# Experts' layer: the last token tile by gathered rows, and one-hots by pairs of tokens

## The chip, the cores and the metric

The kernel runs on one NeuronCore of one Trainium2 chip. The metric is the device time of one execution in microseconds. Before the change the median of three runs is 4340.61 us (4338.75 to 4345.99). TensorE (PE) does the matmuls, VectorE (DVE) and ScalarE (ACT) work on tiles, GpSimd (POOL) does small work here, and SyncE (SP) issues the DMAs.

## The reference

512 tokens of width 1024 pass through one hybrid block (windowed attention beside a state space model), a layer of experts, and then two layers of feed-forward, four-way mixer, feed-forward. The change is in the experts' layer. All is fp32. For each token:

```
q = (h @ w_query)                       8 heads x 256
s1, s2 = q halves . keys                128 scores each, by head
v1, i1 = top 16 of s1;  v2, i2 = top 16 of s2
cand = v1 + v2, all 256 pairs;  sc, ci = top 16 of cand
idx = i1[ci / 16] * 128 + i2[ci % 16]   16 experts of 16384 by head
g = softmax(sc)
act = gelu(peer_u[idx] . h) * g         128 picks for each token
out = sum over picks of act * peer_v[idx]
```

## The kernel before

The experts are not gathered. All 16384 are computed for all tokens, in two dense passes, and a matrix of gates (zero where an expert was not picked) is multiplied in between them. Matmul operands are kept as a rounded high part and a low part, and `three` (lines 352 to 356) does three matmuls for each product: high by high, low by high, high by low.

Weights come as items of 512 KB. `load` (L323, on SP) fetches one into one of three raw buffers, `split_ac` (L335, ScalarE) writes the high part, `split_ve` (L345, VectorE) the low part; six pairs of such parts exist, and splitting runs at most four items ahead of TensorE. Engines run their instructions in the order in which they are written, and wait for semaphores in that order.

`Peer` (line 1814) is the layer. `pe_u`, `ac_u`, `ve_u`, `po_u`, `sp_u` write the first pass for each engine, over 144 items: 16 of the query product (`wq`) and 128 of U (128 experts by 1024). For U item j TensorE makes 24 matmuls with the item's part as weights and all 512 tokens as the moving side, ScalarE puts the GELU of the result in a tile (L1957), and SP stores it to `acts` in HBM (L2114). Beside this VectorE picks: `ve_top` (16 best of 128 keys, by head, half and token tile, 64 times), `ve_cand`, `ve_best` (16 best of 256, 32 times; both use `ve_top16`, L1792 to L1796), `ve_places`, `ve_mark` (indices by comparing and summing), the softmax in `ve_soft` and `ve_norm`. Indices and gates are transposed (`turn`, `ve_turned`), and then `ve_gate` builds for eight tokens at a time one-hot rows in fp16: two comparisons (L2081, L2082) and two products (L2085) over 128 x 1024. TensorE multiplies them token by token (`pe_gate`, L1934, two matmuls of 128 columns after each three U matmuls of an item), ScalarE scales the result into a tile (L1982), and SP stores four gates together to `gates` in HBM. There are 64 such gates.

`schedule` decides in which item each of VectorE's units is written: each item brings a budget of time, each kind of unit has a cost, and units are taken in a fixed order until the budget is used. At most one gate is put in an item. The other engines' parts follow from that list.

`pe_v`, `ac_v`, `ve_v`, `sp_v` write the second pass over 128 items of V (128 experts by 1024). `sp_back` fetches an item's activations, `sp_gc` the gates of four items; `ve_prep` multiplies them (L2182), ScalarE rounds the product (`ac_prep`, L2174), `ve_prep` makes the low part (L2184). TensorE uses the activations of each of four token tiles as weights and V as the moving side, two halves of 512 columns, and sums all items in eight PSUM banks. The last four items (`TAIL`) go tile by tile, and before a tile's last item `TileNorm.pe_turn` turns the tile before, for the feed-forward layer's norm. VectorE adds each finished bank to the residual X (L2211) and runs the norm's part of it.

Of the kernel before, what the change touches and what calls it, by code (L numbers as in the profile page):

```python
# [43 lines left out]
def bc(ap, pos, n):  # L44
# [7 lines left out]
SHARED = {"statistics": ("qvar", "kvar", "aovar", "qsd", "ksd", "aosq", "aosd", "gsq", "gsd", "gss", "sqM", "mvar", "msd"),  # L52
          "operands": ("qn", "kn", "kT", "xM", "xTM", "xMT", "xHM", "xLM", "kv0", "SI", "dt", "mag", "gsub", "gexp", "gg")}
# [13 lines left out]
class Dry:  # L67
# [7 lines left out]
    match_replace = affine_select = iota = dma_start = made  # L75
# [461 lines left out]
class TileNorm:  # L537
# [3 lines left out]
    def __init__(self, k, n, gname, XH, XL, mem):  # L541
        self.k, self.n, self.gname, self.XH, self.XL = k, n, gname, XH, XL
        self.D = [mem[:, 128 * i:128 * i + 128] for i in range(4)]

    def pe_turn(self, i):
        k, n, pe, at = self.k, self.n, self.k.pe, self.k.at
        pe.wait_ge(*at("xD", n, i))
        for j in range(8):

            if i == 3 or j % 4 == 0:  # L550
                b = j if i == 3 else 2 * i + j // 4
                o = k.open(b, b + 1, "xT", n, i, j if i == 3 else j // 4)
            c = 0 if i == 3 else 128 * (j % 4)
            pe.e.matmul(o[:, c:c + 128], k.X[:, i, j * 128:(j + 1) * 128], self.D[i], start=True,  # L554
                        stop=True).then_inc(*pe.up("xT", n, i, "column", j))

    def source(self, i, j):
        if i == 3:
            return self.k.got("xT", self.n, i, j)[:, 0:128]
        return self.k.got("xT", self.n, i, j // 4)[:, 128 * (j % 4):128 * (j % 4) + 128]  # L560
# [13 lines left out]
    def ac_upper(self, i, js):  # L574
        k, n, ac, at = self.k, self.n, self.k.ac, self.k.at
        for j in js:
            ac.wait_ge(*at("xT", n, i, "column", j if i == 3 else js[-1]))
# [16 lines left out]
    def ve_lower(self, i, js):  # L594
        k, n, ve, v, at = self.k, self.n, self.k.ve, self.k.ve.e, self.k.at
        for j in js:

            ve.wait_ge(*at("xH", n, i, j if i == 3 else js[-1]))
# [3 lines left out]
            if i == 3:  # L602
                last.then_inc(*ve.free(("xT", n, i, j)))
                ve.note("xL", n, j)
        if i < 3:
            last.then_inc(*ve.free(("xT", n, i, js[0] // 4)))
# [3 lines left out]
    def ac_tile(self, i, done, mem):  # L610
        if i:
            self.ac_upper(i - 1, range(4))
        self.ac_sums(i, done, mem)
        if i:
            self.ac_upper(i - 1, range(4, 8))
        if i == 3:
            self.ac_upper(3, range(8))

    def ve_tile(self, i):
        self.ve_mean(i)  # L620
        if i:
            self.ve_lower(i - 1, range(4))
        self.ve_diag(i)
        if i:
            self.ve_lower(i - 1, range(4, 8))
        if i == 3:
            self.ve_lower(3, range(8))
# [1185 lines left out]

class Peer:
    def __init__(self, k):
# [3 lines left out]
        ar = k.level(3072)  # L1819
        self.TT = [ar(512) for _ in range(3)]  # L1820
        self.I1T, self.I2T = ar(512, dt=HF), ar(512, dt=HF)
        self.GP = ar(2, 512, dt=HF)
        self.IOX = ar(128, dt=HF)
        ar = k.level(20096)
        self.norm, self.next = TileNorm(k, 1, "n2", self.XH, self.XL, self.TT[0]), None
# [3 lines left out]
        ar.at = 1056  # L1829
# [7 lines left out]
        self.S = [ar(4, 128) for _ in range(16)]  # L1837
        self.TMP = ar(256)
        self.MK = ar(8, 16, 16)
        self.CA = self.KT.rearrange("p a b -> p (a b)").rearrange("p (h k) -> p h k", k=256)  # L1840
        k.close()
        self.gd = k.nc.dram_tensor("gates", (16, 128, 128 * 32), F).ap()
        self.ad = k.nc.dram_tensor("acts", (128, 128, 512), F).ap()
        ar = k.level(16384)
        self.GS = [ar(128, 32) for _ in range(2)]
        self.O1 = [ar(8, 128, dt=HF) for _ in range(4)]
        self.O2 = [ar(8, 128, dt=HF) for _ in range(4)]
        self.RH = [ar(2, 8, 128, dt=HF) for _ in range(4)]
        k.close()
        ar = k.level(2 * 2048 + 6 * 512 + 1024)  # L1850
        self.AH, self.AL = k.rounded("AH", 6, 512), k.rounded("AL", 6, 512)
        self.GC = [ar(16, 4, 32) for _ in range(2)]
        self.AI = [ar(512) for _ in range(6)]
        self.mem = ar(1024)
        k.close(3)
        self.schedule()

# [3 lines left out]
    def schedule(self):  # L1861
        units = [("top", c, i) for c in range(16) for i in range(4)]
        for i in range(4):
            units += [("cand", i)] + [("best", i, h) for h in range(8)] + [("places", i)]
            units += [("soft",)] if i == 3 else []
            units += [("mark", i, 0), ("mark", i, 1)]
        units += [("norm",), ("turned",)] + [("gate", n) for n in range(64)]
        cost = {"top": 1.7, "cand": 2.5, "best": 2.4, "places": 2.5, "soft": 0.8, "mark": 7.0, "norm": 1.9,
                "turned": 4.0, "gate": 4.9}
# [3 lines left out]
        time, turn = 0.0, None  # L1873
        for n, (kind, c) in enumerate(self.items):
            time = min(time, 2.0) + (5.0 if kind == "wq" else 4.2)
            while units and time > 0:
                u = units[0]
                if u[0] == "top" and n < u[1] + 2 or u[0] == "turned" and n < turn + 2:
                    break
                if u[0] == "gate" and self.units[n] and self.units[n][-1][0] == "gate":  # L1880
                    break
                time -= cost[u[0]]
                if u[0] == "gate":
                    time += 2.1
# [6 lines left out]
                self.units[n].append(units.pop(0))  # L1891
        assert not units
        self.loads0 = max(n for n, x in enumerate(self.extras) if x) + 4
        assert self.loads0 < len(self.items) - 1, self.loads0

    def pe_u(self):
        k, pe, at = self.k, self.k.pe, self.k.at
        for n, (kind, c) in enumerate(self.items):
# [4 lines left out]
            else:  # L1903
                gates = [x[1] for x in self.extras[n] if x[0] == "gate"]
                pe_proj(k, (kind, c), self.XH, self.XL, 0, 2,
                        between=partial(self.pe_gate, gates[0]) if gates else None)
                if c == 0:
                    self.pe_scores(15)
            for x in self.extras[n]:
                if x[0] == "turn":  # L1910
                    pe.wait_ge(*at("gg"))
                    for m, src in enumerate((self.E1, self.E2, self.GG)):
                        pe_turn(k, [src[:, i, :, :].rearrange("p h k -> p (h k)") for i in range(4)], 128,
                                ("peT", m), 2, 8)

# [10 lines left out]
    def pe_gate(self, n, t):  # L1926
# [6 lines left out]
        for c in range(2):  # L1933
            last = pe.e.matmul(self.gate_bank[:, 128 * (t % 4):128 * (t % 4) + 128], self.O1[n % 4][:, t, :],  # L1934
                               self.RH[n % 4][:, c, t, :], start=c == 0, stop=c == 1)
# [3 lines left out]
    def ac_u(self):  # L1939
        k, ac, at = self.k, self.k.ac, self.k.at  # L1940
        a = ac.e.activation
        for n, (kind, c) in enumerate(self.items):
# [9 lines left out]
            else:  # L1952
# [4 lines left out]
                a(self.TT[c % 3], k.got(("U", c)), ACT.Gelu).then_inc(*ac.free((("U", c),)))  # L1957
                ac.note("pact", c)
            for x in self.extras[n]:
# [4 lines left out]
                if x[0] == "gate":  # L1964
                    self.ac_gate(x[1])

    def ac_scores(self, c):
        k, ac, at = self.k, self.k.ac, self.k.at
        ac.wait_ge(*at("ps", c))
        ac.e.activation(self.S[c].rearrange("p i k -> p (i k)"), k.got("ps", c),  # L1970
# [15 lines left out]

    def po_u(self):
        k, po, at = self.k, self.k.po, self.k.at
        g = po.e
# [3 lines left out]
        po.after().tensor_copy(self.IOX, self.IO)  # L1993
        g.iota(self.IOI, pattern=[[1, 16]], base=0, channel_multiplier=0).then_inc(*po.up())
        po.after().tensor_copy(self.IOF, self.IOI).then_inc(*po.up("iota"))

    def ve_u(self):
# [3 lines left out]
                "gate": self.ve_gate}  # L2001
# [5 lines left out]
    def ve_top(self, c, i):  # L2007
        k, ve, at = self.k, self.k.ve, self.k.at
        ve.wait_ge(*at("psc", c))
        ve_top16(k, self.S[c][:, i, :], self.V12[:, i, c // 2, c % 2, :], self.IXu[:, i, c // 2, c % 2, :],  # L2010
                 self.TMP[:, 0:128]).then_inc(*ve.up())
# [31 lines left out]

    def ve_soft(self):
# [6 lines left out]
    def ve_norm(self):  # L2051
# [6 lines left out]
        ve.after().tensor_tensor(gg3, gg3, bc(sm, 2, 16), ALU.mult).then_inc(*ve.up("gg"))  # L2058

    def ve_turned(self):  # L2060
        k, ve, v, at = self.k, self.k.ve, self.k.ve.e, self.k.at
        GT, GR = self.QT
        for n, dst in enumerate((self.I1T, self.I2T)):
            ve.wait_ge(*at("peT", n))
            v.tensor_copy(dst, k.got("peT", n)).then_inc(*ve.free(("peT", n)))
        ve.wait_ge(*at("peT", 2))
        v.tensor_scalar(GT, k.got("peT", 2), GSCALE, None, ALU.mult).then_inc(*ve.free(("peT", 2)))
# [5 lines left out]
    def ve_gate(self, n):  # L2073
        k, ve, v, at = self.k, self.k.ve, self.k.ve.e, self.k.at
        o1, o2, rh = self.O1[n % 4], self.O2[n % 4], self.RH[n % 4]
        s = slice(8 * n, 8 * n + 8)
# [1728 lines left out]
```

## Time and profile before

| what | value |
|---|---|
| runs, median of 3 | 4340.61 us |
| profiled execution | span 4340.4 us; the page gives no other time for it |
| granted TensorE clock, mean of the records | 0.960 |
| TensorE busy | 4130.1 us, 95% |
| VectorE busy | 2287.0 us, 53% |
| ScalarE busy | 1404.0 us, 32% |
| GpSimd busy | 189.6 us, 4% |
| DMA | 473.59 MB, mean 109 GB/s |

Busy times of engines overlap. Times are microseconds from the first instruction unless marked ns. A matmul's duration is its passage through the array, and successive ones overlap, so the distance of two starts, not the duration, says what one costs. Instructions are named by the line of the kernel that wrote them, and a helper's line stands for all who call it.

### The profile page before, as it was taken

How to read it: one execution, taken by the hardware profiler on the slowest of the kernel's cores; microseconds unless marked ns; L12 is line 12 of the kernel's file. 1: busy time of each engine (PE TensorE's matmuls, PEld its weight loads, DVE VectorE, ACT ScalarE, POOL GpSimd, SP SyncE). 2: the span in 40 equal slices, each digit the busy share in tenths (PEclk: the TensorE clock that was granted, in tenths of full speed). 3: DMA queues.
4: the chain of work that ended last, by engine and by line, in shares of the span. 5: the costliest groups of instructions: out<-in, count | busy, mean ns of one | idle time of the engine just before them, and what ended most of it. 6: DMA issues, size and time to landing. Idle time of an engine off the chain costs nothing. (4 is left out here: it accounts for less than half of the span.)

```text
span 4340.4 us, 47785 instructions
## 1 busy us (share of the span) xinstructions
PE 4130.1 (95%) x19325; PEld 3249.6 (75%) x19325; DVE 2287.0 (53%) x3707; ACT 1404.0 (32%) x2380; POOL 189.6 (4%) x356
## 2 busy tenths in 40 slices
PE   9789999999999999999999988899999999789999
PEld 7767887666678888888878765788778787657877
DVE  5748888777724444444332776433243338754332
ACT  3444223333333333333222433422232233333221
POOL 8500000000000000000000000000000000000000
PEclk9779999999999999999999987999999999889999
DMA  3012444555566666662332210233323322102332
GB/s 124 1 39 88 127 138 132 178 185 176 177 193 201 189 187 188 190 194 83 94 96 77 78 51 1 73 96 94 97 78 93 97 78 73 36 1 93 97 97 73
DMA packets 253388, 473.59 MB, mean 109 GB/s; under 512 B 15904, under 2 KB 138944, under 8 KB 250992
## 3 DMA queue, kind: packets, MB, share of 16 engines
q1 hardware_dynamic: 253072, 470.45, 35.5%
q8 instruction: 153, 2.51, 0.2%
q14 instruction: 67, 0.55, 0.0%
q10 hardware_dynamic: 96, 0.08, 0.0%
HBM read 399.96 MB, written 70.52 MB: 108 GB/s over the span
## 5 line engine op out<-in xcount | busy, mean ns | idle before, releaser
L345 DVE TENSOR_TENSOR wlast<-wraw,wlast 128x1024 fp32r<-128x1024 f32 x406 | 496.2, 1226 | 762.7 <-ACT wlast L335 762.2
L354 PE MATMUL ps<-XH,wlast 128*128 128x512 f32 (+1 forms) x1888 | 779.5, 413 | 0.0
L356 PE MATMUL ps<-XH,wlast 128*128 128x512 f32 (+1 forms) x1888 | 747.2, 396 | 0.0
L355 PE MATMUL ps<-XL,wlast 128*128 128x512 f32 (+1 forms) x1888 | 746.5, 395 | 0.0
L335 ACT ACTIVATE wlast<-wraw 128x1024 fp32r<-128x1024 f32 x406 | 426.6, 1055 | 403.5 <-PE ps L356 389.2
L345 DVE TENSOR_TENSOR wtwo<-wraw,wtwo 128x1024 fp32r<-128x1024 f32 x212 | 260.1, 1228 | 438.4 <-ACT wtwo L335 437.9
L356 PEld LDWEIGHTS ps<-XH,wlast 128*128 128x128 f32 x1888 | 357.4, 189 | 86.8
L354 PEld LDWEIGHTS ps<-XH,wlast 128*128 128x128 f32 x1888 | 358.1, 190 | 75.4 <-issue 5.2
L355 PEld LDWEIGHTS ps<-XL,wlast 128*128 128x128 f32 x1888 | 358.8, 190 | 70.6
L354 PE MATMUL ps<-XH,wtwo 128*128 128x512 f32 x960 | 397.5, 414 | 0.0
L356 PE MATMUL ps<-XH,wtwo 128*128 128x512 f32 x960 | 381.8, 398 | 0.0
L355 PE MATMUL ps<-XL,wtwo 128*128 128x512 f32 x960 | 381.7, 398 | 0.0
L335 ACT ACTIVATE wtwo<-wraw 128x1024 fp32r<-128x1024 f32 x212 | 223.7, 1056 | 245.4 <-PE ps L356 239.4
L356 PE MATMUL ps<-wlast,AL 128*128 128x512 f32 x672 | 264.7, 394 | 0.0
L355 PE MATMUL ps<-wlast,AH 128*128 128x512 f32 x672 | 263.4, 392 | 0.0
L354 PE MATMUL ps<-wlast,AH 128*128 128x512 f32 x672 | 260.8, 388 | 0.0
L1957 ACT ACTIVATE arena<-ps 128x512 f32<-128x512 f32 x128 | 76.5, 598 | 566.6 <-PE ps L356 566.6
L356 PEld LDWEIGHTS ps<-XH,wtwo 128*128 128x128 f32 x960 | 183.0, 191 | 43.9
L355 PEld LDWEIGHTS ps<-XL,wtwo 128*128 128x128 f32 x960 | 183.9, 192 | 35.7
L354 PEld LDWEIGHTS ps<-XH,wtwo 128*128 128x128 f32 x960 | 183.5, 191 | 35.8
L2336 ACT ACTIVATE HH<-arena 128x512 fp32r<-128x512 f32 x88 | 55.6, 632 | 419.3 <-DVE arena L2354 419.3
L2354 DVE TENSOR_TENSOR arena<-arena,ps 128x512 f32<-128x512 f32 x88 | 60.4, 687 | 245.1 <-PE ps L356 245.1
(476 smaller groups left out, 6801.0 us busy)
## 6 DMA issues: line engine op xcount, KB each, us to landing
wraw<-in_ut SPq DMA_DIRECT2D x128, 512.0 KB, 4.2
wraw<-in_v SPq DMA_DIRECT2D x128, 512.0 KB, 3.9
wraw<-in_ffn_gate SPq DMA_DIRECT2D x88, 512.0 KB, 3.5
wraw<-in_ffn_up SPq DMA_DIRECT2D x88, 512.0 KB, 3.5
wraw<-in_ffn_down SPq DMA_DIRECT2D x88, 512.0 KB, 3.5
acts<-arena SPq DMA_DIRECT2D x128, 256.0 KB, 4.5
gates<-arena SPq DMA_DIRECT2D x16, 2048.0 KB, 9.0
arena<-gates SPq DMA_DIRECT2D x32, 1024.0 KB, 7.9
```

Of the source, the lines that this page charges most:

```text
L335: ac.e.activation(W.items[n][7], W.rawof(n), ACT.Copy).then_inc(*ac.up("whi", n))
L345: ve.e.tensor_tensor(W.items[n][8], W.rawof(n), W.items[n][7], ALU.subtract).then_inc(*ve.up("wlo", n))
L354: mm(out, lh, rh, start=start, stop=False)
L355: mm(out, lh, rl, start=False, stop=False)
L356: return mm(out, ll, rh, start=False, stop=stop)
L1957: a(self.TT[c % 3], k.got(("U", c)), ACT.Gelu).then_inc(*ac.free((("U", c),)))
L2336: a(self.HH[:, f, :], s, ACT.Copy).then_inc(*ac.up("hh", *id, f))
L2354: v.tensor_tensor(s, s, k.got((*id, "up", f)), ALU.mult).then_inc(*ve.free(((*id, "up", f),)))
```

## The change

Three of the four token tiles (384 tokens) stay in the dense passes. The U matmuls go over 384 columns, V uses three tiles of activations, the GELUs, stores and fetches shrink to 384 tokens, and there are 48 gates for 64. The last tile (tokens 384 to 511) is done by its picks: its indices are computed first; GpSimd issues 128 indirect DMAs that fetch for each of the 128 tokens the row of U of its x-th pick (128 rows of 4 KB, 512 KB), and 128 more that fetch the rows of V, into five buffers in turn. VectorE multiplies each row by the token's normalised activations and sums (a "dot", 128 of them); ScalarE takes the GELU in four chunks of 32; VectorE multiplies by the gates and adds each V row, scaled, to one of two accumulators, X itself and `XN` (a "row", 128 of them). One of those 128 only scales its row.

The scores' buffers shrink from 16 to 8. The one-hot rows are laid out by pairs of tokens, [4 pairs, 128, 2], and `O2` is a single buffer. `schedule` has new costs and budgets, puts dots between gates and after them, and a second list (`later`) puts what remains of dots and the rows into the items of the V pass; what is left at the end is written after its last item. In the feed-forward's norm the gathered tile is turned first, before the last item of the first dense tile. Semaphores of some more events are shared by name.

```diff
+DENSE, GATHERED, PICKS = 3, 3, 128
+TOKENS = 128 * DENSE
...
+    ROWS, SCORES, CHUNK = 5, 8, 32
+    GATES = TOKENS // 8
...
+        units = [("top", c, i) for c in range(16) for i in range(4)] + [("rows",)]
+        for i in (GATHERED, 0, 1, 2):
...
+            units += [("index",)] if i == GATHERED else []
+        units += [("norm",), ("turned",)] + [("gate", n) for n in range(self.GATES)]
+        cost = {"top": 1.7, "rows": 1.3, "cand": 2.5, "best": 2.4, "places": 2.5, "soft": 0.8, "mark": 7.0,
+                "index": 0.3, "norm": 2.1, "turned": 3.5, "gate": 2.9, "dot": 1.3}
...
-            time = min(time, 2.0) + (5.0 if kind == "wq" else 4.2)
+            time = min(time, 2.0) + (4.4 if kind == "wq" else 3.0)
...
+                wait = u[0] == "top" and n < u[1] + 2 or u[0] == "turned" and n < turn + 2
+                if wait or u[0] == "gate" and self.units[n] and ("gate", u[1] - 1) in self.units[n]:
+                    u = ("dot", dots)
+                if u[0] == "dot" and (known is None or n < known + 4 or dots == PICKS):
                     break
...
+        later = [("dot", x) for x in range(dots, PICKS)] + [("act", c) for c in range(PICKS // self.CHUNK)]
+        later += [("row", x) for x in range(PICKS)]
...
+            time = min(time, 1.0) + 1.78
...
+                time -= 0.4 if u[0] == "act" else 1.28
...
+        self.later[127] += later
...
+    def pe_expert(self, c, gate):
...
+            last = three(k, o, wh[:, j, :], wl[:, j, :], self.XH[:, j, 0:TOKENS], self.XL[:, j, 0:TOKENS], j == 0,
+                         j == 7)
...
+        for n in range(2 * PICKS):
+            if n >= self.ROWS:
+                m = n - self.ROWS
+                po.wait_ge(*(at("dot", m) if m < PICKS else at("row", m - PICKS)))
+            x = n % PICKS
+            g.indirect_dma_start(out=self.RB[n % self.ROWS], out_offset=None, in_=tables[n // PICKS],
+                                 in_offset=bass.IndirectOffsetOnAxis(ap=self.PLACE[:, x:x + 1], axis=0)).then_inc(
...
+    def ve_dot(self, x):
...
+        ve.wait_ge(*at("gathered", x))
+        ve.wait_ge(*at("xn"))
+        v.tensor_tensor_reduce(out=rows, in0=rows, in1=self.XN, scale=1.0, scalar=0.0, op0=ALU.mult, op1=ALU.add,
+                               accum_out=self.DOT[:, x:x + 1]).then_inc(*ve.up("dot", x))
...
+    def ve_row(self, x):
...
+            acc = self.XN if x % 2 else k.X[:, GATHERED, :]
+            v.scalar_tensor_tensor(acc, rows, w, acc, ALU.mult, ALU.add).then_inc(*ve.up("row", x))
...
+        def pairs(x):
+            return bc(x[:, s].rearrange("p (t u) -> p t u", u=2), 2, 128)
...
+        v.tensor_tensor(o2, io, pairs(self.I2T), ALU.is_equal).then_inc(*ve.up("o2", n))
...
-                if j == 127 and i:
-                    self.next.pe_turn(i - 1)
+                if j == 127:
+                    self.next.pe_turn(self.next.order[i])
...
+            for u in self.later[j]:
+                does[u[0]](*u[1:])
+        x = k.X[:, GATHERED, :]
+        ve.wait_ge(*at("row", PICKS - 1))
```

## Rows read from the trace of the kernel before

**Rows 1.** The page, its busy times and one line of 40 slices in tenths.

```profile
PE 4130.1 (95%) x19325; PEld 3249.6 (75%) x19325; DVE 2287.0 (53%) x3707; ACT 1404.0 (32%) x2380; POOL 189.6 (4%) x356
...
DVE  5748888777724444444332776433243338754332
```

**Rows 2.** Windows: length, busy of each engine (instructions), granted clock, DMA share, GB/s.

```profile
447.00:730.00 283.00, 279.60 (x1214) 222.93 (x1213) 245.15 (x543) 80.87 (x104) 0.00 (x0) 0.99 0.48 136
730.00:1203.00 473.00, 459.62 (x2560) 291.27 (x2560) 361.28 (x313) 161.93 (x257) 0.00 (x0) 1.00 0.55 176
...
1287.00:1990.00 703.00, 703.00 (x3054) 573.25 (x3053) 323.18 (x394) 219.23 (x271) 0.00 (x0) 1.00 0.61 185
```

**Rows 3.** The line of the U pass's GELUs: durations, first and last start.

```profile
L1957 ACT ACTIVATE arena<-ps x128: 597/598/602, 454.8 to 1283.1; 128x512 f32<-128x512 f32 x128
```

**Rows 4.** Order of time in a U item: start, length, instruction.

```profile
560.21 0.40 PE L356 MATMUL ps<-XH,wtwo 128*128 128x512 f32 x1
560.44 0.39 PE L354 MATMUL ps<-XH,wtwo 128*128 128x512 f32 x1
```

**Rows 5.** Order of time in an item with a gate.

```profile
902.44 0.29 PE L1934 MATMUL ps<-arena 128*128 128x128 f16 x2
...
903.33 0.28 PE L1934 MATMUL ps<-arena 128*128 128x128 f16 x2
```

**Rows 6.** Order of time where matmuls are narrower, of 16 and of 256 columns.

```profile
69.94 0.26 PE L354 MATMUL ps<-XH,wtwo 128*128 128x16 f32 x1
...
70.06 0.26 PE L355 MATMUL ps<-XL,wtwo 128*128 128x16 f32 x1
...
2527.91 0.28 PE L354 MATMUL ps<-wlast,XH 128*128 128x256 f32 x1
...
2529.08 0.28 PE L355 MATMUL ps<-wlast,XH 128*128 128x256 f32 x1
```

**Rows 7.** Order of time in the V pass.

```profile
1499.63 0.39 PE L356 MATMUL ps<-wlast,AL 128*128 128x512 f32 x1
1499.86 0.39 PE L354 MATMUL ps<-wlast,AH 128*128 128x512 f32 x1
```

**Rows 8.** VectorE's groups by form: busy, mean ns, idle before; gates, then V pass.

```profile
L2085 DVE TENSOR_TENSOR arena<-arena 128x1024 f16<-128x1024 f16 x106 | 124.8, 1219 | 0.0
...
L345 DVE TENSOR_TENSOR wlast<-wraw,wlast 128x1024 fp32r<-128x1024 f32 x71 | 87.0, 1225 | 161.8 <-ACT wlast L335 161.8
...
L2184 DVE TENSOR_TENSOR AL<-arena,AH 128x512 fp32r<-128x512 f32 x106 | 73.4, 692 | 74.1 <-ACT AH L2174 74.1
```

**Rows 9.** Order of time on VectorE: starts of two successive bests, two successive tops.

```profile
501.75 0.43 DVE L1792 MAX8 arena<-arena 128x8 f32<-128x256 f32 x1
...
504.12 0.43 DVE L1792 MAX8 arena<-arena 128x8 f32<-128x256 f32 x1
...
457.65 0.29 DVE L1792 MAX8 arena<-arena 128x8 f32<-128x128 f32 x1
...
459.35 0.29 DVE L1792 MAX8 arena<-arena 128x8 f32<-128x128 f32 x1
```

**Rows 10.** Waits in the V pass: total us, times, longest.

```profile
DVE AL L2184 <- ACT AH L2174: 74.1, 106, 0.7
```

**Rows 11.** DMA: V pass, 10 us slices of U's gates, 5 us of U, landing, issue.

```profile
q1 hardware_dynamic: 86458, 112.13, 63.1%
...
DMA packets 86486, 112.52 MB, mean 191 GB/s; under 512 B 3855, under 2 KB 59151, under 8 KB 86458
...
GB/s 126 207 202 136 212 184 144 224 168 136 247 159 120 272 154 102 286 154 87 293 154 79 301 146 80 303 143 80 318 129 86 322 118 94 339 94 103 336 88 110
...
817.00:822.00 5.00, 5.00 (x28) 3.06 (x27) 3.13 (x4) 2.52 (x4) 0.00 (x0) 1.00 1.08 455
...
wraw<-in_v SPq DMA_DIRECT2D x107, 512.0 KB, 3.9
...
1501.09 0.33 SPq L323 DMA_DIRECT2D wraw<-in_v  x1
```

More of the change, by code:

```diff
@@ L1836, in __init__ @@
         self.QT = [ar(512) for _ in range(2)]
-        self.S = [ar(4, 128) for _ in range(16)]
+        at_s = ar.at
+        self.S = [ar(4, 128) for _ in range(self.SCORES)]
         self.TMP = ar(256)
+        ar.at = at_s
         self.MK = ar(8, 16, 16)
@@ L1890, in schedule @@
                     self.extras[n].append(u)
-                self.units[n].append(units.pop(0))
+                if u[0] == "index":
+                    known = n
+                if u[0] == "dot":
+                    dots += 1
+                    if dots % self.CHUNK == 0:
+                        self.extras[n + 1].append(("gelu", dots // self.CHUNK - 1))
+                    self.units[n].append(u)
+                else:
+                    self.units[n].append(units.pop(0))
         assert not units
-        self.loads0 = max(n for n, x in enumerate(self.extras) if x) + 4
+        gates = [n for n, x in enumerate(self.extras) if any(u[0] in ("turn", "gate") for u in x)]
+        self.loads0 = max(gates) + 4
         assert self.loads0 < len(self.items) - 1, self.loads0
+        later = [("dot", x) for x in range(dots, PICKS)] + [("act", c) for c in range(PICKS // self.CHUNK)]
+        later += [("row", x) for x in range(PICKS)]
+        self.later, self.gelus, time, gelu = [[] for _ in range(128)], [[] for _ in range(128)], 0.0, 0
+        for j in range(128):
+            time = min(time, 1.0) + 1.78
+            while later and time > 0:
+                u = later[0]
+                if u[0] == "act" and u[1] == PICKS // self.CHUNK - 1 and j < gelu + 2:
+                    break
+                time -= 0.4 if u[0] == "act" else 1.28
+                if u[0] == "dot" and u[1] % self.CHUNK == self.CHUNK - 1:
+                    self.gelus[j].append(u[1] // self.CHUNK)
+                    gelu = j
+                self.later[j].append(later.pop(0))
+        self.later[127] += later
     def pe_u(self):
@@ L2000, in ve_u @@
                 "soft": self.ve_soft, "mark": self.ve_mark, "norm": self.ve_norm, "turned": self.ve_turned,
-                "gate": self.ve_gate}
+                "gate": self.ve_gate, "rows": self.ve_rows, "index": self.ve_index, "dot": self.ve_dot}
         for n, item in enumerate(self.items):
@@ L2147, in pe_v @@
             pe.wait_ge(*at("al", j))
-            for i in range(4):
+            for i in range(DENSE):
                 for n in range(2):
@@ L2153, in pe_v @@
         ws = {j: k.W.pair(("V", j)) for j in range(TAIL, 128)}
-        for i in range(4):
+        for i in range(DENSE):
             for j, w in ws.items():
@@ L2200, in ve_v @@
         k, ve, v, at = self.k, self.k.ve, self.k.ve.e, self.k.at
+        does = {"dot": self.ve_dot, "act": self.ve_act, "row": self.ve_row}
         for j in range(self.LEAD):
@@ L2206, in ve_v @@
                 self.ve_prep(j + self.LEAD)
-        for i in range(4):
+            for u in self.later[j]:
+                does[u[0]](*u[1:])
+        x = k.X[:, GATHERED, :]
+        ve.wait_ge(*at("row", PICKS - 1))
+        for n in range(2):
+            s = slice(512 * n, 512 * n + 512)
+            v.tensor_tensor(x[:, s], x[:, s], self.XN[:, s], ALU.add).then_inc(*ve.up("x+", "peer", GATHERED, n))
+        self.next.ve_tile(0)
+        for i in range(DENSE):
             for n in range(2):
@@ L2266, with __init__ @@
     TAIL = 18
-    def __init__(self, k, name, l, gname, norm, before):
+    def __init__(self, k, name, l, gname, norm, before, order=(0, 1, 2, 3)):
         self.k, self.id, self.norm_n, self.before = k, (name, l), norm, before
@@ L3676, in build @@
         plan_ffn(k, "ffn1", l)
-        stages.append(Ffn(k, "ffn1", l, f"f1{l}", norm, before))
+        stages.append(Ffn(k, "ffn1", l, f"f1{l}", norm, before, (0, 1, 2, 3) if l else (GATHERED, 0, 1, 2)))
         plan_mixer(k, l)
```

232 lines of the change are left out of this document (146 added, 86 removed).

## The prediction

> **What bounds the kernel now.** I read the page's first two parts, then the windows cut at the stages of the experts' layer, then TensorE's order of time inside each stage, and last VectorE's groups, waits and the DMA view of the same stretches. The page gives TensorE 95% and VectorE 53% of the span [rows 1]. By windows, the layer's first expert pass (product with U) is PE-busy at 97 to 99% and the second pass (V, 1287 to 1990 us) at 100%; VectorE has 87% in the picking stretch, 76% in the gates' and 46% in the V pass [rows 2]. So TensorE's stream sets the time everywhere here, with VectorE close behind in the picking stretch. The 128 U items run from the GELU at 454.8 to that at 1283.1: 828.3/127 = 6.52 us each, 835 us in all [rows 3]. A U matmul of 512 columns starts 0.23 us after the one before, 24 x 0.2333 = 5.6 us an item [rows 4]; the 64 items with a gate then take (835 - 64 x 5.6)/64 = 7.45 us, and the order of time shows a step of 0.88 us for three U matmuls and two gate matmuls [rows 5]. V steps at 0.229 us, 5.5 us an item, 704 us for 128 [rows 7].
>
> **TensorE's part.** U keeps 24 matmuls an item, but each goes over 384 columns for 512. No such row exists. Matmuls of 256 columns step at 0.117 us (the two rows are ten starts apart, 1.17 us), and those of 16 columns at 0.112: that is the floor of the weight load [rows 6]. 384 lies above the floor, so I interpolate between 0.117 and 0.2333: 0.175 us, 4.2 us an item (bounds 0.16 and 0.19). V keeps 512 columns and drops a quarter of its matmuls: 18 x 0.229 = 4.13 us an item. 16 gates of 64 go. By TensorE alone: U 80 x 4.2 + 48 x (4.2 + 1.85) = 628 us for 835 (-207); V 529 for 704 (-175). The page "TensorE: Matmul & The Clock Gate" (LDWEIGHTS) of the Trainium skill gives columns/1.2 ns for a weight load, 107 ns here; rows [rows 6] have 112 ns, and by either the load hides under 384 columns.
>
> **VectorE's part, U.** Splitting an item is 1.23 us. The planner's new costs, added up: 64 tops of 1.7 and four times (2.5 + 8 x 2.4 + 2.5 + 2 x 7.0) are 262 us, with the small units 267; 14 query items take 4.4 each, the rest (205) fills U items at 3.0, so picking ends at U 68 and gates 0 to 47 stand at U 69 to U 116, one each. Dots of 1.3: 2 before them, (3.0 + 0.8 - 2.9)/1.3 = 0.7 an item among them, 32 in whole units, and 26 in the last 11 items; 60 in all, and 68 remain for the V pass. Before the gates, its budget of 3.0 plus the split gives 4.23 us an item, as much as TensorE's 4.2. The plan's costs fit what rows show: a top of 128 takes 1.70 us, a best of 256 2.37 [rows 9]. A balance with no slack, and lumps of 7 us (the mark), will leave TensorE waiting now and then; I take 4.4 us for these 69 items: 304 us (bounds 4.2 and 4.7). Gate items: four one-hot operations took 1.22 us each over 1024 fp16 elements [rows 8]; the innermost step of zero becomes a run of two. If that makes VectorE take two elements a step, each costs what 512 elements cost, 0.69 us [rows 8], a gate 2.8 us; with the split and 0.67 dots, 4.8 us, under TensorE's 6.05. If it does not, 1.23 + 4.9 + 0.8 = 6.9 us and 48 x 0.85 = +41 us. I take the fast form. The Trainium skill, "Vector Engine (DVE) Microarchitecture Reference" (Performance modes — why throughput varies by op and dtype), says the pairing mode wants 2-byte operands with step one innermost, and that a single element read again runs at one a cycle: the 1.22 us rows agree with the second half. The gates' operands now lie two elements apart for TensorE; as a full-floor load of 0.112 us each [rows 6], 0.22 a pair where the step now leaves 0.88 - 0.70 = 0.18, they would cost 384 x 0.05 = 19 us, and nothing if the distance does not count; I take 0. The last 11 U items want 2.4 dots each: 56 us with some waiting. U comes to 304 + 291 + 56 = 651, **-184 us**.
>
> **VectorE's part, V.** Per item: the split 1.14 (start to start), multiply and subtract over 384 columns 0.55 each for 0.69 [rows 8], the wait for ScalarE's rounding between them, 74.1/106 = 0.7 now [rows 10], 0.6 then. The plan's 1.78 us an item at 1.28 a unit put 177 units into the 128 items (68 dots, 109 row sums), 1.38 an item. A dot or row sum over 1024 fp32 from two SBUF tiles is like the split, 1.15 to 1.25 us: 1.66. Sum 4.5 us: more than TensorE's 4.13, so VectorE becomes the bound. In its queue the split, multiply and subtract stand behind each gather's wait, and ScalarE's split and TensorE behind those.
>
> **The DMA.** Each gather moves 128 rows of 4 KB, 0.52 MB. A V item carries V 0.52, activations 0.20, gates 0.20 and 1.38 gathers 0.72: 1.64 MB. Now the stage runs 191 GB/s at 63% busy, 302 GB/s if full: 5.4 us. The U pass shows 10 us slices of 339 GB/s (4.8 us) and 5 us at 455 (3.6 us) [rows 11]. The nearest row for 4 KB rows is the slice of 339. With 4.5 by VectorE and 4.8 by DMA I take 4.75 us: 608 us (bounds 4.13 and 5.7).
>
> **The tail.** 19 row sums are left after the last item, and the gathered tile is now the first that TensorE turns: it waits in front of the last item's matmuls for 19 sums x 1.15, two additions and the norm's chain of some 4 us. Nothing covers that, as TensorE is not ahead: **+25 us** (bounds 10 and 60, the latter if gathers pace the sums). V: 608 + 25 for 704, **-71 us**.
>
> **What a gather costs to issue** no row shows. SP issues a transfer in 0.33 us, and one of 512 KB lands 3.9 us after issue [rows 11]. So 0.4 us if descriptors are cheap, 3.9 if gathers do not overlap at all (five buffers say they should), more than that if GpSimd needs long for the 128 places. The plan leaves 608/177 = 3.4 us. I take under 3.1, hidden. The Trainium skill, "SBUF — State Buffer" (Who interferes with whom), speaks against the change: descriptors of a DMA from GpSimd are written by its cores, which share ports with VectorE; it gives 0.62 us alone and 3.1 us beside a VectorE copy. An estimate by that figure: 196 x 3.1 = 608 us for V, the same as mine, and 25 us more in U's last items. No run here shows it yet.
>
> **Sum.** 4340.4 - 184 - 71 = 4085, and about 3 for the index, the normalised row tile (1.2 like a split) and the copy of the gates, which stand in the full picking stretch: **4088 us**. The span of the profiled execution, 4340.4, is the only time the page gives for it; the median run is 4340.61, so I add nothing.
>
> **Rivals.**
> (a) Gathers pace both passes: with g us each, in order on one engine, U's last items take 26g and V 196g in all (19 of them in the tail). The change is 835 - 595 - 26g + 704 - 196g = 944 - 222g us: nothing at 4.25 us, and slower beyond. For it: one issue has 128 places to look up, where SP's 0.33 us deals with one regular block; and each must follow the dot or row five before it. Against: five buffers in flight, and 4.25 us is more than the 3.9 from issue to landing of a transfer of that size. At g = 4.8, 4340 + 122 = 4462. At 3.9 us (serial transfers) 4262.
> (b) The 16 DMA engines become the bound at the stage's present 302 GB/s: V 128 x 5.44 = 696, + 25, so -184 + 17 + 3: 4176. For it: the share of 63% already; against: the 455 GB/s.
> (c) Nothing but TensorE binds: 4340 - 207 - 175 + 25 = 3984. For it: present waits are nearly all other engines' waits for TensorE. Against: the 4.5 us above.
> (d) The pairs do nothing for VectorE: +41, 4129; inside the main range.
>
> **Chances.** Forecast with (d), 4040 to 4140: 0.46. (b) and near it, 4140 to 4220: 0.21. (c), 3960 to 4040: 0.10. Serial gathers, 4220 to 4300: 0.08. (a) slower: 0.13; level: 0.02. This kernel's measurement tells 0.2%, 9 us, from nothing. Faster 0.85, same 0.02, slower 0.13. Range 3990 to 4290: it leaves out (a) and the best of (c).
>
> **What would show it.** After the change: U matmul starts 0.175 us apart; gate operations near 0.69 us; no VectorE wait for gathers in U before its last 11 items; V items of 4.75 us with PE near 87% and VectorE over 90%; a stall of TensorE of some 25 us before the last item, ended by the norm's diagonal; 256 gathers at under 3.1 us. The prediction is wrong if VectorE's top wait in V is a DMA with its steps over 3.4 us, or if U items before the gates exceed 4.7 us.

## The result and the profile after

The changed kernel takes 4078.94 us (median of 4 runs, 4076.54 to 4082.92) against 4339.68 us for the one before (4333.4 to 4345.99): a ratio of 0.9393, 95% interval 0.9377 to 0.9410. The profiled span is 4075.3 us for 4340.4.

First the page after, busy times, VectorE's slices and the DMA's rate; answers to [rows 1].

```profile
PE 3770.3 (93%) x18298; PEld 3085.7 (76%) x18298; DVE 2367.9 (58%) x4034; ACT 1348.4 (33%) x2352; POOL 552.5 (14%) x612
...
DVE  5746898877677888743337764332333266933332
...
GB/s 125 9 26 94 128 190 178 231 285 285 346 354 344 346 353 343 270 88 93 98 78 74 48 1 73 93 93 98 78 94 96 95 75 55 18 37 83 93 99 73
```

The windows after, columns as in [rows 2]: picking, gates, the last U items, V items, the layer's tail.

```profile
447.00:732.00 285.00, 285.00 (x1618) 285.00 (x1617) 259.54 (x586) 101.69 (x140) 6.30 (x5) 1.00 0.57 174
732.00:1030.00 298.00, 297.19 (x2064) 236.64 (x2063) 234.40 (x341) 123.71 (x204) 41.53 (x41) 1.00 0.82 280
1030.00:1085.00 55.00, 33.81 (x175) 32.85 (x173) 30.87 (x47) 11.07 (x16) 26.19 (x20) 0.81 0.97 354
1085.00:1640.00 555.00, 511.66 (x2144) 402.85 (x2145) 447.94 (x590) 175.12 (x240) 250.29 (x162) 0.99 0.97 348
1640.00:1700.00 60.00, 26.00 (x108) 19.47 (x106) 49.71 (x51) 13.26 (x18) 33.96 (x25) 0.80 0.92 330
```

TensorE is still full in the U pass up to 1030 us. In the V pass it has 92%, VectorE 81%, and the DMA engines 97% at 348 GB/s, where the pass before ran at 185 [rows 2]. In the tail TensorE has 43%, and its granted clock is 0.80 on the mean: it fell from 2.4 to 1.2 GHz while TensorE stood (0.51 in 1676 to 1715 us, and still 0.50 in the first matmuls after it, 1718 to 1724).

The lines that bound the passes after: U's GELUs (answers to [rows 3]) and the roundings of V's activations; each with durations, first and last start.

```profile
L2020 ACT ACTIVATE arena<-ps x128: 490/492/495, 453.3 to 1081.3; 128x384 f32<-128x384 f32 x128
...
L2315 ACT ACTIVATE AH<-arena x128: 522/525/527, 1084.3 to 1675.2; 128x384 fp32r<-128x384 f32 x128
```

U items take 628.0/127 = 4.94 us for 6.52, so the pass loses 202 us. V items take 590.9/127 = 4.65 us. From the last GELU to the last addition to X, V pass and tail together, it was 1283.1 to 2001.7 us before and is 1081.3 to 1739.2 after: 61 us less. The two make 263 of the 265 us between the spans.

Matmuls in order of time after, two of U, two of gates; answers to [rows 4, 5].

```profile
600.10 0.34 PE L357 MATMUL ps<-XH,wlast 128*128 128x384 f32 x1
600.28 0.34 PE L358 MATMUL ps<-XL,wlast 128*128 128x384 f32 x1
...
900.19 0.29 PE L1996 MATMUL ps<-arena 128*128 128x128 f16 x2
...
900.90 0.29 PE L1996 MATMUL ps<-arena 128*128 128x128 f16 x2
```

A 384-column matmul starts 0.176 us after the last (ten rows of the same stretch, 600.10 to 601.87). The step with two gate matmuls is 0.71 us, of which the pair takes 0.18, as it did before (0.88 - 0.70).

VectorE's groups from 300 to 1750 us: split, dot, row sum, one-hot, low part (answers to [rows 8]).

```profile
L348 DVE TENSOR_TENSOR wlast<-wraw,wlast 128x1024 fp32r<-128x1024 f32 x185 | 225.2, 1220 | 63.2 <-ACT wlast L338 62.8
L2151 DVE CUSTOM_DVE_ANT_0 arena<-arena 128x1024 f32<-128x1024 f32 x128 | 154.3, 1221 | 8.3 <-DMA arena<-in_u,arena 8.2
...
L2174 DVE SCALAR_TENSOR_TENSOR X<-arena,X 128x1024 f32<-128x1024 f32 x64 | 82.0, 1281 | 2.5 <-DMA arena<-in_v,arena 2.4
...
L2325 DVE TENSOR_TENSOR AL<-arena,AH 128x384 fp32r<-128x384 f32 x128 | 71.5, 559 | 75.6 <-ACT AH L2315 75.6
...
L2225 DVE TENSOR_TENSOR arena<-arena 128x1024 f16<-128x1024 f16 x96 | 61.8, 686 | 0.0
```

The one-hot operation fell from 1219 to 686 ns. VectorE waited for gathered rows 8.2 us in all dots and 7.0 in all row sums: they come in time.

TensorE's waits from 1000 to 1740 us: what waited, for whom, us in total, times, longest.

```profile
PE ps L357 <- DVE AL L2325: 53.9, 52, 4.4
PE ps L558 <- DVE arena L590: 45.3, 1, 45.3
PE ps L357 <- ACT arena L2020: 17.4, 2, 16.8
```

Three costs are new: V items held by VectorE's low parts, the norm's first turn (L558) behind the row sums, and one stop near the end of the U pass.

That V queue in order of time, an item with one row sum and an item with two:

```profile
1640.58 1.22 DVE L348 TENSOR_TENSOR wtwo<-wraw,wtwo 128x1024 fp32r<-128x1024 f32 x1
...
1641.71 0.55 DVE L2323 TENSOR_TENSOR arena<-arena 128x384 f32<-128x384 f32 x1
...
1642.85 0.56 DVE L2325 TENSOR_TENSOR AL<-arena,AH 128x384 fp32r<-128x384 f32 x1 [0.59 <-ACT AH L2315]
1643.33 1.28 DVE L2174 SCALAR_TENSOR_TENSOR X<-arena,X 128x1024 f32<-128x1024 f32 x1
1644.53 1.22 DVE L348 TENSOR_TENSOR wlast<-wraw,wlast 128x1024 fp32r<-128x1024 f32 x1
...
1647.28 1.28 DVE L2174 SCALAR_TENSOR_TENSOR arena<-arena 128x1024 f32<-128x1024 f32 x1
1648.47 1.28 DVE L2174 SCALAR_TENSOR_TENSOR X<-arena,X 128x1024 f32<-128x1024 f32 x1
1649.67 1.22 DVE L348 TENSOR_TENSOR wlast<-wraw,wlast 128x1024 fp32r<-128x1024 f32 x1
```

From split to split: 3.95 us with one sum, 5.14 with two, so at 1.38 an item 3.95 + 0.38 x 1.19 = 4.40 us without any wait for a DMA. The items take 4.65. The rest is a wait for a DMA, and not one for gathered rows. VectorE's longest waits from 1000 to 1740 us:

```profile
DVE AL L2325 <- ACT AH L2315: 75.6, 128, 0.6
DVE arena L2323 <- DMA arena<-acts: 36.4, 25, 3.4
```

The first is in the 4.40 already. The second, for the activations that SP fetches, is 36.4/128 = 0.28 us an item, and 4.40 + 0.28 = 4.68: full DMA engines reach TensorE through VectorE's queue.

The DMA view from 1150 to 1700 us (queues with packets, MB, share of 16 engines; landings), answers to [rows 11]:

```profile
q1 hardware_dynamic: 74126, 102.29, 53.7%
q0 software_dynamic: 23986, 87.33, 42.8%
...
wraw<-in_v SPq DMA_DIRECT2D x108, 512.0 KB, 7.1
...
arena<-in_v,arena POOLq DMA_INDIRECT x123, 7.6
```

### The profile page after: what moved, and what is told of

Read it like the earlier page. It is cut to its first block and busy times, and to the rows that moved or that the text cites. A ratio compares the mean times of both kernels' runs of the same rounds, so it can differ in the third digit from the quotient of the medians.

```text
span 4075.3 us, 46458 instructions
## 1 busy us (share of the span) xinstructions
PE 3770.3 (93%) x18298; PEld 3085.7 (76%) x18298; DVE 2367.9 (58%) x4034; ACT 1348.4 (33%) x2352; POOL 552.5 (14%) x612
## 5 line engine op out<-in xcount | busy, mean ns | idle before, releaser
L357 PE MATMUL ps<-XH,wlast 128*128 128x512 f32 (+2 forms) x1888 | 734.0, 389 | 17.4 <-ACT arena L2020 17.4
L359 PE MATMUL ps<-XH,wlast 128*128 128x512 f32 (+2 forms) x1888 | 708.4, 375 | 0.0
L358 PE MATMUL ps<-XL,wlast 128*128 128x512 f32 (+2 forms) x1888 | 707.8, 375 | 0.0
L357 PE MATMUL ps<-XH,wtwo 128*128 128x512 f32 (+1 forms) x960 | 374.5, 390 | 0.0
L358 PE MATMUL ps<-XL,wtwo 128*128 128x512 f32 (+1 forms) x960 | 362.5, 378 | 0.0
L359 PE MATMUL ps<-XH,wtwo 128*128 128x512 f32 (+1 forms) x960 | 362.2, 377 | 0.0
L2080 POOL DMA_INDIRECT arena<-in_u,arena x128 | 172.0, 1344 | 783.7 <-DVE arena L2151 547.1
L357 PE MATMUL ps<-wlast,AH 128*128 128x512 f32 x504 | 202.2, 401 | 33.2 <-DVE AL L2325 33.1
L2080 POOL DMA_INDIRECT arena<-in_v,arena x128 | 193.8, 1514 | 212.2 <-DVE X L2174 99.3
L2315 ACT ACTIVATE AH<-arena 128x384 fp32r<-128x384 f32 x128 | 67.2, 525 | 402.2 <-DVE arena L2323 402.2
```

The source lines that it names most:

```text
L357: mm(out, lh, rh, start=start, stop=False)
L358: mm(out, lh, rl, start=False, stop=False)
L359: return mm(out, ll, rh, start=False, stop=stop)
L2080: g.indirect_dma_start(out=self.RB[n % self.ROWS], out_offset=None, in_=tables[n // PICKS], in_offset=bass.IndirectOffsetOnAxis(ap=self.PL ...
L2315: ac.e.activation(self.AH[:, j % 6, :], self.AI[j % 6], ACT.Copy).then_inc(*ac.up("ah", j))
```

## The experiments

Three theories stood for V items of 4.65 us: VectorE's queue, the DMA engines, or GpSimd's gathers. Each edit is against the changed kernel unless it says otherwise.

**Without the gathered tile's work.** No gathers; the dots and row sums are left out, and one memset clears the dots' results.

```diff
-        for n in range(2 * PICKS):
+        for n in range(0):
...
-        v.tensor_tensor_reduce(out=rows, in0=rows, in1=self.XN, ...)
-            v.scalar_tensor_tensor(acc, rows, w, acc, ...)
+        ve.note("row", x)
```

> The changed kernel without its gathers, dots and row sums: the last token tile gets nothing from its experts. This is TensorE's own gain. If only TensorE binds where nothing else does, the V items fall from 4.65 us (first to last rounding of the activations, 1084.3 to 1675.2 us) to 18 x 0.229 = 4.13, 66 us less; the 45 us stall before the norm's first turn goes to under 5; the 17 us stall at the end of the U pass, where SP sends eight fetches in a row, shrinks to under 8 if the gathers' bytes cause it and stays at 17 if the fetches alone do. Sum: 4079 - 66 - 42 - 10 = about 3960 us. Rival: V items stay over 4.4 us because of SP's own transfers or VectorE's multiply and subtract; then about 3990.

Measured: 3947.4 us, ratio to before 0.9100 (0.9074 to 0.9126). The first to the last rounding in V is 1064.2 to 1579.2, 4.06 us an item, and 4.15 between items 16 and 112: TensorE's pace. The stop of 16.8 us is gone, and the norm's waits are 4.2 us. So a quarter off the dense passes is worth 392 us, and the picks' own work gives 132 us back.

**Narrow V rows.** The same number of gathers, a quarter of the bytes.

```diff
-        tables = (k.d["u"], k.d["v"].rearrange("a b d -> (a b) d"))
+        tables = (k.d["u"], k.d["v"].rearrange("a b (q d) -> (a b q) d", q=4))
...
-            g.indirect_dma_start(out=self.RB[n % self.ROWS], ...
+            cut = 1024 if n < PICKS else 256
+            g.indirect_dma_start(out=self.RB[n % self.ROWS][:, 0:cut], ...
```

> The V rows are gathered 256 columns wide instead of 1024 (from a view of V in which the same indices fall on other quarter rows); as many gathers of 128 rows, as many row sums over 1024 columns, the gathered tile's sums are of stale data. The DMA engines carry 1.09 gathers' worth of bytes less an item once rows begin. Theory DMA (16 DMA engines bound the V items, 1.64 MB at 353 GB/s = 4.65 us): V items with rows fall to TensorE's 4.13 or VectorE's 4.4; the second half of the V pass gains 0.3 to 0.5 us an item, 80 items: 25 to 40 us, and the tail's stall 5 to 15 us: 4025 to 4050. Theory VectorE (split, multiply, wait for ScalarE, subtract, 1.38 dots or rows in one queue = 4.4 us, and only 0.26 of 4.65 is waiting for DMA): gains at most 0.26 x 80 = 21 us and nothing in the tail, whose 24 sums are VectorE's own: 4058 to 4070. Theory GpSimd (each gather 1.5 us of descriptor work paces): no change, 4079.

**Narrow row sums.** Full gathers, sums over 256 columns.

```diff
+        rows = rows[:, 0:256]
...
-            acc = self.XN if x % 2 else k.X[:, GATHERED, :]
+            acc = (self.XN if x % 2 else k.X[:, GATHERED, :])[:, 0:256]
```

> Row sums over 256 columns for 1024, gathers unchanged: the gathered tile's result lacks the rest. A row sum falls from 1.28 to about 0.45 us. Theory VectorE: its queue falls from 4.4 to 3.3 us in items with rows, so TensorE's 4.13 or the DMA takes over; 80 items gain 0.3 to 0.5 us, 25 to 40 us, and the tail of 24 sums loses 15 to 20 us: 4020 to 4040. Theory DMA: the V items stay at 4.65 us and the tail, paced by gathers of 0.52 MB, gains under 8: 4070 to 4079. Theory GpSimd: no change.

**Both.**

> The two edits narrow_rows and narrow_sums together: V rows gathered 256 wide, sums over 256 columns. Each alone took V items in the half with row sums from 4.75 to 4.4 and 4.5 to 4.7 us. Theory two bounds side by side (VectorE's queue 4.4, the DMA engines about 4.6): with both gone the items with row sums fall to TensorE's 4.15, as without gathers, 75 items x 0.27 below narrow_rows, and the norm's stall of 36 us to 15: 4050 - 20 - 20 = 4010. Rival: GpSimd's 128 indices a gather (1.5 us each) or latency paces the rest; then items stay at 4.4 and the total at 4035 to 4045.

Windows in the half of the V pass with row sums (from 1340 us), one line from each kernel: as changed, narrow rows, narrow sums, both. Where VectorE waits there for the activations' fetch, that row stands below; with narrow rows it has none, and with both it has waited 3.1 us in all.

```profile
1340.00:1640.00 300.00, 273.12 (x1145) 213.71 (x1144) 244.10 (x280) 94.29 (x128) 138.27 (x89) 0.99 0.98 350
...
DVE arena L2323 <- DMA arena<-acts: 18.0, 14, 3.4
```

```profile
1340.00:1640.00 300.00, 289.22 (x1227) 228.16 (x1226) 259.81 (x299) 100.23 (x136) 149.88 (x95) 1.00 0.81 250
```

```profile
1340.00:1640.00 300.00, 281.25 (x1174) 223.57 (x1174) 183.59 (x288) 96.66 (x132) 122.21 (x92) 0.98 1.00 360
...
DVE arena L2324 <- DMA arena<-acts: 77.2, 28, 7.2
```

```profile
1340.00:1600.00 260.00, 260.00 (x1131) 211.97 (x1130) 181.49 (x286) 100.60 (x129) 104.45 (x91) 1.00 0.88 277
```

Measured: narrow rows 4049.4 us (0.9334, 0.9312 to 0.9356), narrow sums 4050.5 (0.9338, 0.9313 to 0.9364), both 4014.2 (0.9241, 0.9225 to 0.9256). Narrow rows came out at the edge of the DMA theory's forecast, and narrow sums between the forecasts of the two theories, so neither holds alone. Over sixteen items at a time, from the starts of the roundings, items 64 to 112 take 4.74 to 4.76 us as changed; with narrow rows 4.40 to 4.47, VectorE's sum of 4.40; with narrow sums 4.44 to 4.71 under DMA engines that are full at 360 GB/s; with both 4.14 to 4.15 from item 80 on, and TensorE busy for the whole window.

VectorE's time confirms it. With narrow rows, 259.8 us busy and 40.2 us of waits for ScalarE's rounding fill the 300 us: nothing is left for a DMA. With narrow sums it has 183.6 us of work and waits 77.2 us for activations. Each edit alone stops at the other bound. So VectorE's queue (4.4) and the DMA engines (about 4.6) lie side by side; that the changed kernel's 4.74 is a little more than the longer because the two alternate is argued, not shown. For the V items the theory of GpSimd falls: 91 gathers of 128 rows each in 260 us did not hold TensorE.

In the tail it does not fall. TensorE's longest wait there is 45.3 us as changed, 36.1 with narrow rows, 38.0 with narrow sums and still 26.8 with both, where 15 was forecast. With both, GpSimd issues one gather behind the other:

```profile
1634.12 0.95 POOL L2081 DMA_INDIRECT arena<-in_v,arena  x1 [0.30 <-issue]
1635.37 0.95 POOL L2081 DMA_INDIRECT arena<-in_v,arena  x1 [0.31 <-issue]
```

That is 1.25 us each, and from 1629 us on VectorE's sums of 0.48 us follow at that pace and wait 14.6 us for rows. So the sums behind the last item have three bounds near each other: VectorE's 1.19 us, GpSimd's 1.25, and the bytes', by an estimate from 0.52 MB at the 350 GB/s above, 1.5.

**Two buffers for five.**

```diff
-    ROWS, SCORES, CHUNK = 5, 8, 32
+    ROWS, SCORES, CHUNK = 2, 8, 32
```

> Two gather buffers for five, so that at most two gathers are under way. From issue to landing they take 7.6 us in the V pass, 1.5 us of it on GpSimd; with the sum's 1.3 us two buffers give one gather each (7.6 + 1.3)/2 = 4.5 us, less if the DMA engines are emptier, about 3.8. By rival (a) of the prediction, gathers pace the passes at g us each and the change is 944 - 222 g: at 3.8 a gain of 100 (4240), at 4.5 a loss of 55 (4395). If that rival's sum is right the time lies at 4240 to 4395 and V items at 5.2 to 6.2 us. If the five buffers were not what hid the latency, within 20 us of 4079.

Measured: 4296.1 us, 0.9886 (0.9864 to 0.9908). VectorE's waits from 1100 to 1900 us:

```profile
DVE arena L2151 <- DMA arena<-in_u,arena: 84.9, 39, 5.7
DVE AL L2325 <- ACT AH L2315: 75.5, 128, 0.6
DVE arena L2174 <- DMA arena<-in_v,arena: 67.8, 37, 5.0
DVE X L2174 <- DMA arena<-in_v,arena: 60.4, 32, 4.9
```

Now the gathers pace the pass: 151 of them in 650 us, 4.30 us each, V items of 5.86 us, the DMA engines down to 83%. GpSimd was busy for only 34% of that stretch; it waited for the two buffers. The prediction's formula gives 944 - 222 x 4.3 = -11, no gain; 45 us were left. The U pass makes the difference: 647 us where the formula has 707, as its items were shorter than I took them (below) and the last eleven took 82.5 us and not 26 x 4.3 = 112. V pass and tail lost 141 us, and the formula has 139. So rival (a)'s sum is right for V, with a g that five buffers keep away.

**Gathered tile last, some sums between the dense tiles' additions.**

```diff
-                if j == 127:
-                    self.next.pe_turn(self.next.order[i])
+                if j == 127 and i:
+                    self.next.pe_turn(i - 1)
...
-        self.later[127] += later
+        self.rest = later
...
+        rest = list(self.rest)
+        for i in range(DENSE):
+            for u in rest[0:3]:
+                does[u[0]](*u[1:])
+            rest = rest[3:]
```

> The gathered tile is turned last as before the change, with three leftover row sums ahead of each dense tile's addition and ten behind the last. Nothing else differs. If the 45.3 us wait of TensorE for the norm's diagonal is a cost of the order, the tail costs 45 less and the ten sums behind the last tile plus the norm's chain, 10 x 1.3 + 7 = 20 us, come in its place: 25 us faster, about 4054. If the gathers pace the leftover sums (2.5 us each), the sums ahead of each tile delay VectorE's additions and the gain is under 10 us: 4070.

Measured: 4049.9 us, 0.9335 (0.9299 to 0.9371), 29 us faster in the medians. Its four runs lie between 4039.9 and 4066.6 us, so the size of the gain is loose, some 16 us either way; the profiled run is 22 us faster than that of the changed kernel. TensorE's wait for the diagonal falls from 45.3 us to 28.4 in all, the longest 16.8.

**SP's fetches spread.**

```diff
-                for c in range(2):
-                    self.sp_gc(c)
-                for j in range(self.BACK):
+                self.sp_gc(0)
+            if n > self.loads0:
+                for j in self.backs.get(n - self.loads0, ()):
                     self.sp_back(j)
+                if n == self.loads0 + 4:
+                    self.sp_gc(1)
...
+    backs = {1: (0,), 2: (1,), 3: (2,), 5: (3,), 6: (4,)}
```

> SP's eight fetches before the V pass (two of gates, six of activations, written in one block) are spread over the last U items, one an item; all else as changed. Theory: their block is what keeps the activations' store behind it and ScalarE and TensorE for 16.8 us; so 12 to 17 us faster, 4063. Rival: the DMA engines are full there anyway (0.97 of 1030 to 1085 us), the bytes are the same, and the wait only moves into the first V items: within 5 us, 4075 to 4079.

Measured: 4064.8 us, 0.9361 (0.9345 to 0.9377), 14 us faster. TensorE's wait for ScalarE's GELUs falls from 17.4 to 10.3 us, not to nothing, the last eleven U items take 61.6 us for 68.6, and the V items 4.59 for 4.65. The block is seen on SP's queue in the changed kernel, and ScalarE behind it:

```profile
1040.66 8.30 SPq L2262 DMA_DIRECT2D arena<-gates  x2
1049.01 11.32 SPq L2270 DMA_DIRECT2D arena<-acts  x6
...
1060.86 0.43 SPq L2255 DMA_DIRECT2D acts<-arena  x1
...
1069.45 0.49 ACT L2020 ACTIVATE arena<-ps 128x384 f32<-128x384 f32 x1 [19.76 <-DMA acts<-arena]
```

The store at 1060.86 stood behind the block, ScalarE's GELU behind the store, TensorE behind the GELU. Each row of the view adds up several issues. Taken singly, the second fetch of gates held SP for 7.9 us and the first of activations for 6.3; the other five took 0.5 to 1.3, where the median issue takes 0.4. The same two stall in the kernel before (3.0 and 3.6 us) and without the gathered tile's work (1.3 and 4.4), and cost TensorE nothing there, so the loss needs both the block and the gathers. DMA engines that are merely full do not do it: in the V pass, at 97%, 110 of 114 fetches of activations were issued in under 1 us. What holds these two was not tried.

**Plain one-hots** in the changed kernel, and **pairs alone** in the kernel before.

```diff
-            return bc(x[:, s].rearrange("p (t u) -> p t u", u=2), 2, 128)
-        io = bc(self.IOX, 1, 4)
+            return bc(x[:, s], 2, 128)
+        io = bc(self.IOX, 1, 8)
```

> The changed kernel with the one-hots laid out as before, single tokens with a repeated element innermost; the planner's costs stay. Each of four operations a gate goes back to 1.22 us. Prediction (d): VectorE's queue in a gate item is 1.23 + 4.9 + 0.8 = 6.9 us against TensorE's 5.68 as measured (70th to 116th GELU, 261.4 us for 46): 48 x 1.2 = 59 us slower, 4138; by the prediction's own 6.05 it was 41 us. Rival: the gates run ahead in four buffers and VectorE has room in the last items, so part of it is absorbed: 20 to 30 us. Rival: two elements apart costs TensorE, so that going back gives some of it back.

> The kernel before with nothing but the one-hots by pairs. Its gate items take 7.37 us (69th to 111th GELU, 309.5 us for 42) of which TensorE's matmuls take 8 x 0.88 = 7.04; the rest is TensorE waiting for one-hots. Theory: VectorE falls from 6.1 to 4.0 us an item, the waits go, and 64 x 0.3 = 15 to 20 us is gained: 4322. Rival: strided fp16 operands slow TensorE's gate matmuls by up to 0.05 us a pair, 26 us lost, which cancels it: 4340 or above.

Measured: plain in the changed kernel 4130.6 us (0.9504, 0.9486 to 0.9521), 52 us slower than with pairs; a gate item takes 6.75 us ((1075.2 - 764.5)/46), VectorE's 6.9 nearly. Pairs in the kernel before 4314.2 (0.9942, 0.9925 to 0.9958), 29 us faster. TensorE's waits for one-hots there, first before, then with pairs:

```profile
PE ps L1934 <- DVE arena L2085: 16.8, 32, 3.4
```

```profile
PE ps L1934 <- DVE arena L2091: 1.3, 1, 1.3
```

Its gate items fall from 7.37 to 7.04 us (309.4 and 295.7 us for 42), the step with two gate matmuls stays at 0.88. So operands two elements apart cost TensorE nothing that shows.

**More dots beside the gates**, and combinations.

```diff
-                    time += 0.8
+                    time += 1.4
```

> One number of the planner: a gate item gives back 1.4 us of budget, not 0.8, so 1.15 dots stand beside a gate for 0.67. 82 dots are in the U pass for 60, the V pass has 174 units, none is left after its last item, and the last stand in item 125. VectorE in a gate item: 1.23 + 2.8 + 1.15 x 1.3 = 5.5 us under 5.68; DMA there 280 GB/s + 40. If each unit taken out of the full V pass is worth its VectorE or DMA time, the stall of 45 us before the norm goes to 5 or 10 (five sums and a chain), V items stay at 4.65: 4040. Rival: gate items become VectorE's or the DMA's and lengthen by 0.2 to 0.4 us: 4050 to 4060.

> spread and order_last together: 4079 - 14 - 29 = 4036 if they are independent; 4050 if the same DMA bytes or the same sums stand behind both.

> spread, order_last and more_dots together. more_dots leaves no sums after the last item, so order_last then has little left to take off: 4025 to 4030 if the U pass hides 22 more dots; 4040 if gate items lengthen.

Measured: more dots 4040.6 us (0.9308, 0.9293 to 0.9324); spread with the tile last 4060.9 (0.9357, 0.9341 to 0.9373); all three 4030.5 (0.9287, 0.9271 to 0.9302), 48 us under the changed kernel. With more dots gate items stay at 5.69 us, the V items at 4.62, and the norm's longest wait is 10.0 us: 22 dots were free in the U pass. Spread and tile last did not add up, as 29 + 14 would be 4036, and 4060.9 is above both forecasts. V's last rounding starts at 1663.4 us with both and at 1663.8 with the tile last alone, though it began 5.6 us sooner; I read this as bytes moved off one stretch that met full engines in the next, and no run shows it. The two kernels have the same code from there on. The profile with both is 6 us longer, in the stretch from 2200 to 2700 us, where TensorE's granted clock is 0.89 for 0.91; and the 11 us between the medians lies within the 27 us over which the runs with the tile last alone scatter.

## Why the prediction was right

Forecast 4088 us, measured 4078.9: -252 forecast on the span, -265 measured. By its own steps:

- **384 columns at 0.175 us.** 0.176. Right, interpolated between 256 and 512 columns, above the 0.112 us that 16 columns take.
- **VectorE with no slack in picking, 4.4 us an item.** Mis-sized: first to 69th GELU 287.3 us for 68 items, 4.22, TensorE's own. VectorE was 91% busy and held nothing up: TensorE has no wait for it from 447 to 732 us. That the lumps of 7 us were absorbed by the items split ahead is my reading. 12 us too dear over 69 items.
- **Gate items 6.05 us.** Measured 5.68. I had carried 1.85 us from the items before, which held waits for one-hots; the eight pairs are 8 x 0.18 = 1.44, and the experiment on the kernel before shows the rest to be waits (7.04 for 7.37). 18 us too dear.
- **Pairs halve the one-hots.** 686 ns for the forecast 0.69 us, and rival (d) at 41 us measured 52, since TensorE needs less than I took. The price of operands two elements apart, taken as 0, was 0; by its own 0.22 - 0.18 it would have been 15 us, not 19. The Trainium skill's page named there, "Vector Engine (DVE) Microarchitecture Reference" (Performance modes — why throughput varies by op and dtype), agrees with both rows.
- **Last eleven items 56 us.** From the 117th GELU on 68.6 us (1012.6 to 1081.3), 13 too cheap. Without the gathered tile's work they take 48.3, and with SP's fetches spread 61.6: of the 20 us, 7 are the block's, and 13 come with the gathers' work even so. A wait that I had not named; the fetches stood in the code. About 3 us of it are the clock: after the stop 18 matmuls start 0.32 us apart and not 0.176, at a granted clock of 0.50 (1.2 GHz).
- **V items 4.75 us between VectorE's 4.5 and the DMA's 4.8.** 4.65, and both bounds are shown. VectorE's 4.40; the DMA engines carry 1.64 MB at 348 to 360 GB/s in 4.6 to 4.7 us. Rival (b)'s 302 GB/s came from dividing by a busy share, and the share does not scale that way: [rows 11] had the better row in its slices.
- **Tail 25 us.** 45.3. The five sums of the last four items stood behind the last low part too, so 24 sums and not 19, and they ran at 1.63 us (1675.8 to 1714.9), fed at 306 GB/s, not at VectorE's 1.15. VectorE alone takes 1.19, and from 1693 to 1709 us GpSimd issued ten gathers without waiting for anything, 1.65 us each. Whether GpSimd or the bytes set that pace is open; with both narrow edits GpSimd alone sets it, at 1.25. The bounds held it.
- **Gathers under 3.1 us, hidden.** GpSimd takes 1.34 and 1.51 us of its own for one, and in the passes five in flight come at the pace of use. In the tail they are not hidden where the bytes are few. The 3.1 us do not appear: 0.93 to 2.45 us are all there are. I had also taken the Trainium skill for saying more than it does. Its page "SBUF — State Buffer" gives 3.1 us beside a `tensor_copy` (A bandwidth-pool intuition that's wrong), and says that `tensor_tensor` did not stall such a DMA (Who interferes with whom). Here VectorE's splits and products are such `tensor_tensor` operations, and its dots and row sums have two inputs as well; no run here has a copy beside the gathers.
- **Rival (c), TensorE alone, 3984.** Without the picks' work 3947. Its sum for U is 626 us, not 628 (80 x 4.2 + 48 x 6.05); its gate items carried 18 us of waits, and its tail 25 us of row sums, of which 4.2 are left there.
- **The signs.** TensorE was to be near 87% and VectorE over 90% busy in the V pass; they are 92% and 81%. The second sign went against the prediction's own sum, where 3.9 of 4.75 us are work and 0.6 a wait for ScalarE.

U was 18 us too dear (picking 12, gates 18, less 13 in the last items). V was 10 us too cheap (the tail 20, less 12 in the items, and small terms). Part of the closeness is luck: errors of both signs met.

## What to carry over

Taking work off the bound engine is worth what that engine shows, up to the next bound, and here two of those (VectorE's queue and the DMA engines) lay within 5% of each other, so that easing one alone gave half. Work handed to spare engines should be placed where both it and its bytes are free: 22 dots moved from the full second pass into the first gained 38 us by one number. A rival that falls in the long pass can still bind in a short stretch where nothing covers it, as GpSimd's issuing did in the tail with both edits. Before an in-order queue sends a block of transfers, ask which store stands behind it, and before a reordered tile is waited for first, count every unit that is written ahead of it.

## What the runs showed that I had not expected

The DMA engines hold 345 to 360 GB/s for hundreds of microseconds on a mix in which 62319 of 98140 packets are under 2 KB and the rows lie wherever the picks fall, where the same stage had looked 63% full at 191. A gather of 128 rows of 4 KB occupies GpSimd for 0.93 us at the least and up to 2.45; in the V pass both 0.94 and 1.68 us are common, and what makes the difference was not tried. And a single issue on SP can take 6.3 and 7.9 us for 0.4, right behind a fetch of gates (768 KB), while the same engines at 97% in the V pass leave issues at 0.4: the queue that issues becomes a place to wait, and a busy share does not say when.
